# A decoder block on one Trainium2 core: sparse-attention stage with V stationary and transposed outputs, modulation vectors on GpSimd, stick-breaking logits issued a row ahead

## The reference

```python
def _stick_breaking_attention(q, k, v):
...
        log_1m_beta = jnp.where(causal, jax.nn.log_sigmoid(-z), 0.0)
        tail = lax.cumsum(log_1m_beta, axis=3, reverse=True) - log_1m_beta
        A = jnp.where(causal, jnp.exp(jax.nn.log_sigmoid(z) + tail), 0.0)
        outs.append(jnp.einsum('bhts,bshd->bthd', A.astype(v.dtype), v[:, :end]))
...
def _dsa_attention(q, k, v, q_idx, k_idx, w_idx, slopes, topk):
...
        _, sel = lax.top_k(score, topk)
...
        logits = logits - slopes[None, :, None, None] * dist[:, None]
        logits = jnp.where(valid[:, None], logits, -jnp.inf)
        p = jax.nn.softmax(logits, axis=-1)
        return jnp.einsum('bhtk,btkd->bthd', p.astype(v.dtype), v_sel)
...
    o = jnp.concatenate([_rmsnorm(o_sb.reshape(B, S, SB_WIDTH), sb_out_gain),
                         _rmsnorm(o_dsa.reshape(B, S, DSA_WIDTH), dsa_out_gain)], axis=-1)
    return o @ w_o
...
        mod = c_act @ w_mod[l] + b_mod[l]
        sh1, sc1, g1, sh2, sc2, g2 = jnp.split(mod, 6, axis=-1)
        h = _modulate(_rmsnorm(x, norm1_gain[l]), sh1, sc1)
        x = x + g1[:, None, :] * _hybrid_mixer(h, ...)
        h = _modulate(_rmsnorm(x, norm2_gain[l]), sh2, sc2)
        x = x + g2[:, None, :] * _swiglu(h, w_gate[l], w_up[l], w_down[l])
    sh_f, sc_f = jnp.split(c_act @ w_mod_final + b_mod_final, 2, axis=-1)
    return _modulate(_rmsnorm(x, final_gain), sh_f, sc_f)
```

## Time and profile before

| | |
|---|---|
| runs | 1785.08, 1784.23, 1784.81 us; median 1784.81 |
| profiled execution | 1785.24 us |
| its span | 1783.5 us |
| busy: PE, PEld, DVE, ACT, POOL | 83%, 68%, 53%, 34%, 30% |
| mean granted TensorE clock | 0.904 of full speed |
| stages 0 to 5 | 64.7, 362.6, 222.9, 213.85, 140.6, 778.9 us |

### The profile page before, as it was taken

The page is one execution under the profiler, slowest core; times in us unless marked ns, Lnnn a source line. Parts: engine busy times, 40 slices in busy tenths (PEclk is TensorE's granted clock), DMA queues, the critical chain, the costliest instruction groups (busy, mean ns, idle before and its releaser), DMA issues. The chain is left out here.

```text
span 1783.5 us, 20750 instructions
## 1 busy us (share of the span) xinstructions
PE 1473.6 (83%) x6865; PEld 1212.3 (68%) x6865; DVE 951.8 (53%) x1688; ACT 607.3 (34%) x1066; POOL 528.8 (30%) x298
## 2 busy tenths in 40 slices
PE   1579988691777758888479689999999999999996
PEld 1457866571656647778258568888888888888884
DVE  5307799995676648988672343223223223223326
ACT  4325655541676645666311340210210111111102
POOL 1141322331433339990410221321321321321214
PEclk9789889895898879889579889999999999999998
DMA  7150233244423235530410311111210210210102
GB/s 283 33 130 1 71 106 106 87 136 119 100 65 78 48 131 194 194 124 19 165 36 1 100 54 48 52 51 39 67 50 24 71 47 24 71 47 24 47 0 94
DMA packets 107274, 139.70 MB, mean 78 GB/s; under 512 B 5704, under 2 KB 79514, under 8 KB 107231
## 3 DMA queue, kind: packets, MB, share of 16 engines
q1 hardware_dynamic: 107232, 139.18, 25.5%
HBM read 114.77 MB, written 20.99 MB: 76 GB/s over the span
## 5 line engine op out<-in xcount | busy, mean ns | idle before, releaser
L1746 DVE TENSOR_TENSOR act_full<-silu_gate,ps_up 128x512 f32<-128x512 f32 x44 | 30.3, 688 | 388.0 <-ACT silu_gate L1605 388.0
L1759 DVE TENSOR_TENSOR x<-ps_down,x 128x512 f32<-128x512 f32 x176 | 120.0, 690 | 96.9 <-PE ps_down L1719 96.9
L1659 POOL TENSOR_TENSOR wgu_lo<-wgu_raw,wgu_hi 128x2048 fp32r<-128x2048 f32 x22 | 101.4, 4611 | 231.8 <-ACT wgu_hi L1600 231.8
L281 PE MATMUL ps_proj<-hTh,win_hi 128*128 128x512 f32 (+1 forms) x336 | 111.6, 415 | 47.0 <-POOL win_lo L544 46.8
L1663 POOL TENSOR_TENSOR wd_lo<-wd_raw,wd_hi 128x2048 fp32r<-128x2048 f32 x11 | 50.6, 4604 | 326.3 <-ACT wd_hi L1610 326.3
L1719 PE MATMUL ps_down<-wd_hi,act_hi 128*128 128x512 f32 x352 | 139.6, 397 | 2.7 <-DVE x L1759 2.7
L1719 PE MATMUL ps_down<-wd_hi,act_lo 128*128 128x512 f32 x352 | 139.5, 396 | 0.0
L1719 PE MATMUL ps_down<-wd_lo,act_hi 128*128 128x512 f32 x352 | 139.4, 396 | 0.0
L1707 PE MATMUL ps_gate<-h2T_hi,wgu_hi 128*128 128x512 f32 x352 | 137.2, 390 | 0.0
L1707 PE MATMUL ps_gate<-h2T_hi,wgu_lo 128*128 128x512 f32 x352 | 137.0, 389 | 0.0
L1707 PE MATMUL ps_up<-h2T_hi,wgu_lo 128*128 128x512 f32 x352 | 137.0, 389 | 0.0
(11 more groups left out here) (251 smaller groups left out, 3641.6 us busy)
## 6 DMA issues: line engine op xcount, KB each, us to landing
wmod_b<-in_w_mod_dram SPq DMA_DIRECT2D x8, 1536.0 KB, 7.1
wgu_raw<-in_w_gate_dram SPq DMA_DIRECT2D x22, 512.0 KB, 4.0
wgu_raw<-in_w_up_dram SPq DMA_DIRECT2D x22, 512.0 KB, 5.3
wd_raw<-in_w_down_dram SPq DMA_DIRECT2D x11, 1024.0 KB, 4.9
win_raw<-in_w_in_dram SPq DMA_DIRECT2D x20, 512.0 KB, 4.4
wm<-in_w_mod_dram SPq DMA_DIRECT2D x4, 2048.0 KB, 11.4
scr_qkv<-proj_hi SPq DMA_DIRECT2D x16, 512.0 KB, 2.6
scr_qkv<-proj_lo SPq DMA_DIRECT2D x16, 512.0 KB, 3.0
```

Source lines behind the costliest of these rows:

```text
L281: last = pe.matmul(ps[:, s], w[:, t, :], x[:, t, s], start=(t == 0 and w is wh and x is xh), stop=(t == KD - 1 and w is wl))
L1659: pool.tensor_tensor(wl[:, m], wr[:, m], wh[:, m].bitcast(F32), ALU.subtract).then_inc(wlr, 1)
L1746: dve.tensor_tensor(af[:, u % 2], sg[:, u % 2], ps_u[:, u % 2], ALU.mult).then_inc(gat, 1)
L1759: dve.tensor_tensor(g.x1[:, i, half(c)], ps_d[:, n % 4], g.x1[:, i, half(c)], ALU.add).then_inc(add, 1)
```

## The change

- **Stage 0**: b_mod_final and final_gain are loaded as two more groups of `vec`; one constant goes.
- **Stage 1**: w_mod_final's products come here, before the indexer's logits: eight loads of 1 MB on SP between the others, into the place of `score`; 32 products on DVE, 16 column sums on PE, three small DVE operations, and a store of the two final vectors. PE waits for the sums' first use before the indexer's logits, and POOL for the products before it writes to `score`.
- **Stage 2**: PE issues the logits of row r + 1 before the transposes of step r; `a_rows` becomes two tiles, and a slot is free when its own row is transposed. POOL has one operation of w_mod's chunks 0 to 3 behind each `a_rows` (32 products, 28 additions, 512 columns).
- **Stage 3**: the same plan (`attention_plan(5)`) as stage 2, unrolled, rows from i = 0 to 7: V is stationary, the probabilities move, and the output is transposed (`o_dT`). The reciprocals of four rows' sums become a diagonal on POOL, a matmul with ones spreads it, ACT copies it, and POOL normalises once for 512 columns. POOL has the chunks 4 to 7 here, DVE none. w_o is loaded in this stage. The sums and rows at the end go.
- **Stage 4**: PE first sums the chunks to columns and spreads the gates; the biases come by broadcast. Squares are on ACT, additions on DVE, the reciprocal roots of four blocks go in one diagonal, and the scaling multiplies out of PSUM. DVE and POOL share the low parts. y(0) to y(2) run with their hh and lh products before any hl one; the others as before. `ps_y` has 3 slots, not 4.
- **Stage 5**: gate 2 is in SBUF already.

```diff
@@ phase1: SP's loads, PE's sums, DVE's products
                 load(0, 0)
                 load(0, 1)
+                load_final(0)
+                load_final(1)
...
+                load_final(6)
+                load_final(7)
                 double_k()
                 load(0, 5)
+                sp.wait_ge(fcr, 3)
+                sp.dma_start(vecs.rearrange("r (t p) -> p (r t)", p=P), fin[:], allow_slow_non_contiguous=True).then_inc(fst, 16)
...
                 pe.wait_ge(wtk, 1)
+                pe.wait_ge(fmd, 4 * NF)
+                for n in range(2 * KD):
+                    last = pe.matmul(ps_s[:, 1, n:n + 1], facc[n // 4][:, P * (n % 4):P * (n % 4) + P], g.ones[:, 0:1],
+                                     start=(n == 0), stop=True, skip_group_check=True)
+                last.then_inc(fcm, 1)
+                pe.wait_ge(fcr, 1)
...
+                for n in range(NF):
+                    dve.wait_ge(fwl[n % 2], 16 * (n // 2 + 1))
+                    for x in range(4):
+                        t = 4 * (n % 2) + x
+                        if t == 0:
+                            ins = dve.tensor_scalar(facc[n // 2], fw[:, n % 2, x], g.csil[:, 0:1], None, ALU.mult)
+                        else:
+                            dve.wait_ge(fmd, 4 * n + x)
+                            ins = dve.scalar_tensor_tensor(out=facc[n // 2], in0=fw[:, n % 2, x], scalar=g.csil[:, t:t + 1],
+                                                           in1=facc[n // 2], op0=ALU.mult, op1=ALU.add)
@@ phase2: POOL, PE
-                    if r % 4 == 0 and gr >= 2:
-                        pool.wait_ge(td, done_by[gr - 2])
-                    pool.tensor_tensor(a[:, gr % 2, r % 4, 0:w], bt[:, r % NB, 0:w],
+                    if gr >= 2:
+                        pool.wait_ge(td, row_done(gr - 2, r % 4))
+                    pool.tensor_tensor(a[gr % 2][:, r % 4, 0:w], bt[:, r % NB, 0:w],
                                        pb[:, r % NPB, WIDE - w + 1:WIDE + 1], ALU.mult).then_inc(mul, 1)
+                    n, m = r // 8, r % 8 // 2
+                    if r % 2 == 0:
+                        product(n, m)
+                    elif n % 2 or m:
+                        add(n, m)
+                        added += 1
...
+                logits(0)
                 for r in range(len(of_step)):
...
+                    if r + 1 < NR:
+                        logits(r + 1)
@@ phase3, new: POOL
+                for gr in range(NG):
+                    for x in range(2):
+                        n, m = gr // 2, 2 * (gr % 2) + x
+                        product(n, m)
+                        if n % 2 or m:
+                            add(n, m)
+                            added += 1
+                    if gr >= 2 and (gr - 2) % 4 >= 2:
+                        normalise(gr - 2)
+                    diagonal(gr)
@@ phase3, new: ACT
+                for r in range(len(of_step)):
+                    if r < NR:
+                        w, gr = P * (rows[r][1] + 1), r // 4
+                        act.wait_ge(tt, r + 1)
+                        if gr >= 2:
+                            act.wait_ge(td, row_done(gr - 2, r % 4))
+                        act.activation(a[gr % 2][:, r % 4, 0:w], nl[:, r % NL, 0:w], ACT.Exp, scale=-1.0,
+                                       bias=nm[:, r % NL:r % NL + 1], accum_out=sm[:, r:r + 1]).then_inc(ex, 1)
+                    for n in of_step[r]:
+                        s = slice(left(n), HALF)
+                        act.wait_ge(td, n + 1)
+                        if n >= NA:
+                            act.wait_ge(vd, n - NA + 1)
+                        act.activation(ah[:, n % NA, s], tr[:, slot["u", n] % 2, s], ACT.Copy).then_inc(ahr, 1)
@@ phase3, new: DVE
+                for r in range(len(of_step)):
+                    if r < NR:
+                        h, i = rows[r]
+                        w = P * (i + 1)
+                        dve.wait_ge(zr, r + 1)
+                        if r >= NL:
+                            dve.wait_ge(ex, r - NL + 1)
+                        dve.tensor_tensor_reduce(nl[:, r % NL, 0:w], z[:, r % 2, 0:w], g.score[:, soff(i):soff(i + 1)],
+                                                 g.nslope[:, h:h + 1], 3e38, ALU.add, ALU.min,
+                                                 nm[:, r % NL:r % NL + 1]).then_inc(tt, 1)
+                    for n in of_step[r]:
+                        s = slice(left(n), HALF)
+                        dve.wait_ge(ahr, n + 1)
+                        dve.tensor_tensor(al[:, n % NA, s], tr[:, slot["u", n] % 2, s], ah[:, n % NA, s].bitcast(F32),
+                                          ALU.subtract).then_inc(alr, 1)
@@ phase3, new: PE, behind each step
+                    for gr in ends[r - 2] if r >= 2 else ():
+                        t = free_slot(("s", gr))
+                        pe.wait_ge(dgr, gr + 1)
+                        pe.matmul(tr[:, t], g.ones[:], dg[:].rearrange("p b n -> p (b n)"), start=True,
+                                  stop=True).then_inc(sd, 1)
@@ phase4, new: POOL, PE, DVE
+                rstd(0)
+                w_lo(0)
+                rstd(1)
+                w_lo(1)
+                o_lo(0)
+                for t in range(2, KD):
+                    w_lo(t)
+                o_lo(1)
...
+                for n in range(NY):
+                    y(n, ("hh", "lh"), True, False)
+                for n in range(NY):
+                    y(n, ("hl",), False, True).then_inc(ym, 1)
+                for n in range(NY, 2 * NT):
...
+                add_squares(0)
+                variance(0)
+                add_squares(1)
+                variance(1)
+                diagonals(0)
+                diagonals(1)
+                scale(0)
...
+                scale(1)
+                dve.wait_ge(olp, KD)
+                for n in range(2 * NT):
+                    i, c = n // 2, n % 2
+                    gate(n, i, c)
+                    residual(n, i, c)
```

More of the change, by code:

```diff
@@ L790, in phase2 @@
     WIDE = SEQ
+    NMOD = 8
     with ExitStack() as ctx:
@@ L1255, in _, with free_slot @@
-                for c, r, half, ps in rows:
-                    if c == len(mods) - 1:
-                        pe.wait_ge(mbs, 1)
-                    pe.matmul(ps, g.ones[:, 0:1], acc[:, c], start=True, stop=True).then_inc(rowm, 1)
-def phase4(nc, k, g, A, vecs):
+                def free_slot(e):
+                    n = slot[e] - 2
+                    if n >= 0:
+                        kind, x = events[n]
+                        pe.wait_ge(sc if kind == "s" else alr, x + 1)
+                    return slot[e] % 2
@@ new lines, in logits @@
+                def logits(r):
+                    h, i = rows[r]
+                    w, j = P * (i + 1), h % 2
+                    if i == 0:
+                        pe.wait_ge(loaded[j], 32 * (h // 2 + 1))
+                    if r >= 2:
+                        pe.wait_ge(tt, r - 1)
+                    q = qs[:, j, P * i:P * i + P]
+                    for c in range(0, w, HALF):
+                        x = slice(c, min(c + HALF, w))
+                        pe.matmul(z[:, r % 2, x], q, g.kdh[:, x], start=True, stop=False)
+                        last = pe.matmul(z[:, r % 2, x], q, g.kdl[:, x], start=False, stop=True)
+                    last.then_inc(zr, 1)
@@ L1396, in _ @@
-                for h in range(2):
-                    sum_sb(h)
+                    for s in range(2):
+                        n = 2 * h + s
+                        pe.wait_ge(dgr, n + 1)
+                        if n == 3:
+                            pe.wait_ge(gbr, 4)
+                        pe.matmul(ps_r[:, n], g.ones[:], dg[:].rearrange("p b n -> p (b n)"), start=True,
+                                  stop=True).then_inc(spr, 1)
+                sums(0)
+                sums(1)
                 spread(0)
-                transposes(0)
```

845 lines of the change are left out of this document (393 added, 452 removed).

## The result

The changed kernel took 1801.33 us (median of 4 runs, 1799.3 to 1804.24) against 1784.94 us before: a ratio of 1.0091, 95% interval 1.0073 to 1.0108. It is slower by 16.4 us; the forecast was 21, with 1780 to 1832 as its range. The profiled execution took 1800.85 us, its span is 1798.9 us, 15.4 more than before.

What follows compares the result with a forecast made beforehand. Waits between engines were taken to decide stages 2 and 4, DVE to bound stage 3's rows before the change. Stages 0 to 4 gave 0.6 + 2.6 - 9.6 + 26.4 + 1.0 = +21.0, so 1806 us, range 1780 to 1832.

Steps and rivals of the forecast that it cites:

- three tiny operations: Stage 1: three tiny DVE operations for the final vectors before the indexer logits, given no cost of their own.
- the sums and logits: Stage 1: 3 us of ACT's work hide most of PE's column sums, not the logits behind them: +1.4 us.
- its mechanism: Stage 2: logits a row ahead remove ACT's wait for z; 2.6 less 1.4 lost gives 1.2 us a head, -9.6.
- The 1.4 us a head: Stage 2: lost because PE's in-order transposes now stand behind next-row logits that wait for a scan.
- GpSimd hidden: Stage 2: POOL's 60 new operations at 1.2 us, 72 us in all, fit its spare time: cost 0.
- the chain as described: Stage 3: neg_logits, exp, pT_hi and pT_lo of a row follow one another without overlap: 27.1 us a head.
- 217 in all: Stage 3: eight heads at 27.1 us; with start, end and barrier 240.3 against 213.85, +26.4.
- the chain that I had named: Stage 4: scale(0)'s low parts out at 46, six wo_lo to 60, four low parts, gate(0) at 67; stage +1.0 us.
- B: Rival, stage 2: waits removed by the early logits all paid out, -46 instead of -9.6, kernel 1770 us; chance 0.12.
- C: Rival, stage 3: the supposed chain overlaps, ACT's 16 us a head, 88 us less, kernel 1718 us; chance 0.04.
- D: Rival, stage 1: DMA queue makes the key copies late, +10, kernel 1816 us; chance 0.11.
- E: Rival: low clock in stage 3 and blocked diagonals in stage 4, 26 us more, kernel 1832 us; chance 0.11.

Runs made afterwards that it cites:

- e2: Changed kernel with stage 2's logits of row r back at the start of step r: 1812.92 us, stage 2 222.5 us.
- e5: Changed kernel with PE's transposes of step r ahead of the logits of row r + 1 in stage 2: 1799.64 us, stage 2 209.2 us.
- e3: Changed kernel with GpSimd's w_mod products and additions in stages 2 and 3 cut to 16 of 512 columns, except each chunk's first product: 1803.27 us, single run.
- e1: Changed kernel with VectorE computing neg_logits(r + 1) ahead of the pT_lo of step r in stage 3: 1741.18 us, stage 3 166.7 us.
- e1b: Changed kernel with ScalarE making pT_hi of step r ahead of the exponential of row r in stage 3: 1752.54 us, stage 3 179.3 us.
- e8: Changed kernel with no wo_lo on GpSimd ahead of its first low parts in stage 4: 1805.38 us in a single run, stage 4 147.6 us.
- e4: Changed kernel with all eight wo_hi ahead of oT_hi on ScalarE and wo_lo(2), (3) ahead of GpSimd's first low parts in stage 4: 1801.49 us.

## Why the prediction was right, and where not

- **Stage 0 and 1: right in sum, the parts partly by luck.** The two loads cost 0.6. ACT's copy of the weight tile waited longer for its load, and starts at 113.10 instead of 110.36; less the 0.6, this is 2.1 us where I put 1.2:

```profile
113.10 1.06 ACT L464 ACTIVATE win_hi<-win_raw 128x1024 fp32r<-128x1024 f32 x1 [10.58 <-DMA win_raw<-in_w_in_dram]
```

  Then PE's sums and the logits behind them, two of DVE's rows, the second its first score operation, and what POOL had beside the first:

```profile
128.79 3.63 PE L650 MATMUL ps_score<-ones,mod_acc_final 128*128 128x1 f32 x32
132.68 0.44 PE L663 MATMUL ps_score<-kidx_hi,qidx_stack 128*128 128x384 f32 x1 [0.27 <-DVE final_cols L707]
...
132.66 2.22 DVE L709 TENSOR_SCALAR final_cols<-final_cols 128x8 f32<-128x8 f32 x1
...
135.03 0.61 DVE L717 TENSOR_SCALAR score<-relu,wtok 128x384 f32<-128x384 f32 x1
...
132.50 2.36 POOL L580 TENSOR_TENSOR lat_lo<-proj_full,lat_hi 128x1024 fp32r<-128x1024 f32 x1
```

  And POOL's same operation in the kernel before:

```profile
130.09 2.36 POOL L552 TENSOR_TENSOR lat_lo<-proj_full,lat_hi 128x1024 fp32r<-128x1024 f32 x1
```

  The sums take 3.63 us, as forecast. DVE starts its scores at 135.03, 4.9 us later than before, because one of the "three tiny operations", on 8 columns, took 2.22 us beside POOL's operation. But before, the first score operation itself met POOL's operation and took 2.56 us; now it takes 0.61. It ends at 135.64 instead of 132.68, 3.0 later, as forecast. Of these 3.0, 0.6 are stage 0's and 2.1 the load's, so the sums and logits added only 0.2 where I had 1.4: too little for the load and too much for the sums cancelled.
- **Stage 2: right in its mechanism, its sum partly by luck.** -8.9 against -9.6. The wait for logits went as said, one for transposes took its place as said, and e2 shows that without the early logits the gain is gone. But from last scan to last scan a head gained 1.5 us (25.5 to 24.0) and not 1.2, and the stage's start and end, which I had left out, lost 1.8: 29.7 us to the first head's last scan instead of 29.0, and 16.4 behind the last one instead of 15.4. The 1.4 us a head that I took to be lost to the order on PE are not borne out: e5 gave a steady head some 0.2 back.
- **GpSimd hidden: right** (e3). Its products took 1.04 us and its additions 1.27; I had 1.2 for both.
- **Stage 3, the head: right.** 27.5 us against 27.1, by the chain as described; e1 and e1b each open it and take 62.5 and 50 us away.
- **Stage 3, the sum: wrong by 11.** The step that failed is "217 in all", eight heads at 27.1. The chain has all its members only from the row on in which there are units to transpose, five rows behind the first. From the first neg_logits at 649.46 to the first one of 1024 columns at 661.19 it took 11.7 us, where I had 27.1 less the last row's 3.3, 23.8: 12.1 too much. I had counted the full pipeline in the first head and its emptying at the end as well. Against that, seven heads were 2.5 us too cheap; the end behind the start of the last row, 873.28 - 853.3 = 20.0, was 1.4 shorter than the 21.4 of the forecast.
- **Stage 4: +6.1 against +1.0; the order of events right, prices too low.** y starts 41.15 us into the stage and not 37, and the first gate product comes at 69.9 and not 67. Up to the last addition of the first half (17.4 us) all is as forecast; the diagonals start at 28.1 and scale(0) at 38.9, 10.7 later and not 7: a diagonal, its spread of two records and the handover take 2.9 us at a granted clock of 0.55 in that stretch, and one diagonal 1.5 more. The collisions with wo_lo, 2.2 in the additions and 1.5 in the diagonal, are measured by e8, in which y starts at 37.5; I had set 2 in all. Behind that lies the chain that I had named: POOL's low parts are out at 48.4 and not 46, its six wo_lo take 15.1 us and not 14, its four low parts of the second half 6.5 and not 6. And y(3) to y(15) took 73.1 us, 5.62 per 24 matmuls at a granted clock of 1.00, while I had used stage 5's 5.44: 2.4 us. No row of y in the kernel before would have told me: there 336 of its 384 matmuls, behind the last transposes, fill this stretch,

```profile
925.31:1001.80 76.49, 76.44 (x339) 62.96 (x337) 24.10 (x38) 9.43 (x16) 0.00 (x0) 1.00 0.00 1
```

  and start 0.2267 us apart (925.62 to 1001.36), 5.44 per 24. In the changed kernel the same products start 0.2333 apart (944.3 to 1016.6), and so they do in every experiment here. Why is open.
- The Trainium skill's rule on interference ("SBUF — State Buffer", "Who interferes with whom"), of which the prediction asked what the new diagonals would pay: with two inputs in SBUF they do wait for GpSimd's wo_lo, 2.18 and 2.81 us in e4, and so do the additions. POOL's power on 8 columns, which reads SBUF too, held up none of the additions in e8, so there the rule says more than was measured. The scalings with one input in PSUM took 0.70 us each beside wo_lo, as it says. That DVE's additions, not only the diagonals, have two inputs in SBUF I had overlooked.
- **The rivals.** B, the removed waits of stage 2 paid out, would have been -46; the stage gave 8.9, with 51.9 us of new waits for the transposes. C, overlap in stage 3, is what e1 makes of it, not what the change did. D did not happen: the key copies were issued at 116 to 120, and DVE's first score operation ended 3.0 us later. Of E one diagonal was blocked, 1.5 us; the spreads in stage 3 cost about what was forecast (from the end of pT_lo at 754.44 to the next neg_logits at 757.02 it is 2.6 us, forecast 2.4, at a granted clock of 1.00).

The errors of stage 3 (-11) and stage 4 (+5) have opposite signs; that the total was missed by only 5 us is in part luck.

## What to carry to other kernels

Where two in-order engines hand a row to and fro, write down the loop "which operation stands behind which" before counting anyone's work: here VectorE lost a third of its work and the stage became longer, because a producer that had run a row ahead now stood behind a consumer. Moving that producer one place up, on either engine, was worth 62 and 50 us, more than the whole rewrite moved. When such a chain is priced, count the rows in which all its members are present, not all rows; and before GpSimd's spare time is filled, look at what VectorE does at that moment.
